# Second normalisation moved behind the up projection, early modulation products in row halves, and two groups of late modulation moved forward

## What is computed

```python
mod = cs @ w_mod[li] + b_mod[li]
sh_a, sc_a, gt_a, sh_f, sc_f, gt_f = [m[:, None, :] for m in jnp.split(mod, 6, axis=-1)]
h = rmsnorm(x, g_attn[li]) * (1.0 + sc_a) + sh_a
z = h @ w_in[li]
...
o = jnp.concatenate([oa.reshape(b, t, A_VW), ob.reshape(b, t, B_QW)], axis=-1) @ w_out[li]
x = x + gt_a * o
h2 = rmsnorm(x, g_ffn[li]) * (1.0 + sc_f) + sh_f
...
f, cnew = conv_ffn(h2, cstate, w_up[li], conv_w[li], conv_b[li], w_down[li])
...
x = x + gt_f * f
```

## Time and profile before

| | |
|---|---|
| median of the runs | 2734.76 us |
| the profiled execution's own time | 2732.63 us |
| its span, first to last instruction | 2730.9 us |
| TensorE matmul busy | 2620.5 us (96%) |
| VectorE (DVE) busy | 1558.8 us (57%) |
| ScalarE (ACT) busy | 957.5 us (35%) |
| GpSimd (POOL) busy | 544.7 us (20%) |
| mean granted TensorE clock | 0.985 of full speed |

### The profile page before, as it was taken

One profiled execution on the slowest core, in us unless ns is written; L12 is line 12 of the kernel. 1 busy time (PEld: TensorE's weight loads), 2 busy tenths in 40 slices (PEclk: granted clock), 3 DMA queues, 4 the chain that ended last, 5 costly groups with the idle time before them and its releaser, 6 DMA issues.

```text
span 2730.9 us, 50066 instructions
## 1 busy us (share of the span) xinstructions
PE 2620.5 (96%) x19783; PEld 2445.0 (90%) x19783; DVE 1558.8 (57%) x2873; ACT 957.5 (35%) x1974; POOL 544.7 (20%) x477
## 2 busy tenths in 40 slices
PE   7999999999999996999999999999999999999997
PEld 2268889898988995999999999999999999999997
DVE  1369889864457887854443544444444444345454
ACT  2236666654344336422222222222222222222224
POOL 1057777751003543310000000000000000000003
PEclk9999999999999998999999999999999999999998
DMA  8866556551216652533323232332332233232321
GB/s 291 294 202 184 184 174 183 182 145 51 66 40 188 169 165 70 155 108 93 93 79 93 81 90 82 90 88 83 93 92 72 87 93 91 81 93 79 93 93 69
DMA packets 416205, 324.91 MB, mean 119 GB/s; under 512 B 44410, under 2 KB 360218, under 8 KB 414880
## 3 DMA queue, kind: packets, MB, share of 16 engines
q1 hardware_dynamic: 410032, 302.55, 37.3%
q0 software_dynamic: 5248, 14.56, 1.7%
q10 hardware_dynamic: 688, 4.47, 0.4%
HBM read 307.67 MB, written 14.07 MB: 118 GB/s over the span
## 4 chain that ended last, share of the span: by engine, by line
PE 81%; DVE 8%; DMA 3%; issue 3%; POOL 2%; ACT 2%; SPq 1%; ACTq 0%; DVEq 0%; POOLq 0%
PE ps L1565 24%; PE ps L1567 23%; PE ps L1566 23%; DVE late_f L1261 3%; PE ps L1539 3%; PE ps L1654 2%; PE ps L1620 2%; DMA w_raw<-in_w_mod 2%; DMA w_raw<-in_w_out 2%; POOL oT L696 1%; PE ps L1638 1%; SPq L536 1%; DVE oT L1261 1%; ACT w_hi L798 1%; PE ps L1576 1%
## 5 line engine op out<-in xcount | busy, mean ns | idle before, releaser
L1565 PE MATMUL ps<-x_hi,w_hi 128*128 128x272 f32 x4480 | 1319.0, 294 | 53.7 <-DVE w_lo L1155 24.7
L1567 PE MATMUL ps<-x_hi,w_lo 128*128 128x272 f32 x4480 | 1302.9, 291 | 0.0
L1566 PE MATMUL ps<-x_lo,w_hi 128*128 128x272 f32 x4480 | 1293.5, 289 | 0.0
L1565 PEld LDWEIGHTS ps<-x_hi,w_hi 128*128 128x128 f32 x4480 | 850.3, 190 | 72.5 <-issue 32.2
L1566 PEld LDWEIGHTS ps<-x_lo,w_hi 128*128 128x128 f32 x4480 | 851.7, 190 | 0.0
L1567 PEld LDWEIGHTS ps<-x_hi,w_lo 128*128 128x128 f32 x4480 | 849.0, 190 | 0.0
L1155 DVE TENSOR_TENSOR w_lo<-w_raw,w_hi 128x1024 fp32r<-128x1024 f32 x368 | 459.0, 1276 | 341.0 <-ACT w_hi L798 340.6
L798 ACT ACTIVATE w_hi<-w_raw 128x1024 fp32r<-128x1024 f32 x368 | 375.6, 1056 | 715.3 <-PE ps L1567 574.1
L1566 PE MATMUL ps<-y_lo,w_hi 128*128 128x272 f32 x1408 | 407.2, 289 | 0.0
L1565 PE MATMUL ps<-y_hi,w_hi 128*128 128x272 f32 x1408 | 405.8, 288 | 0.0
L1567 PE MATMUL ps<-y_hi,w_lo 128*128 128x272 f32 x1408 | 405.0, 288 | 0.0
(11 more groups left out here) (194 smaller groups left out, 2081.6 us busy)
## 6 DMA issues: line engine op xcount, KB each, us to landing
w_raw<-in_w_mod SPq DMA_DIRECT2D x192, 512.0 KB, 4.6
w_raw<-in_w_up SPq DMA_DIRECT2D x176, 512.0 KB, 4.4
w_raw<-in_w_down SPq DMA_DIRECT2D x88, 512.0 KB, 4.7
w_raw<-in_w_in SPq DMA_DIRECT2D x56, 512.0 KB, 3.9
w_raw<-in_w_in SPq DMA_DIRECT2D x32, 256.0 KB, 3.7
w_raw<-in_w_out SPq DMA_DIRECT2D x16, 512.0 KB, 5.5
w_raw<-in_w_out SPq DMA_DIRECT2D x64, 128.0 KB, 3.9
x_transposed<-xT SPq DMA_DIRECT2D x4, 1088.0 KB, 8.1
```

What stands on the lines that cost most here:

```text
L1565: pe.matmul(out[:, 0:n], hi_w, hi_x, start=first, stop=False)
L1566: pe.matmul(out[:, 0:n], hi_w, lo_x, start=False, stop=False)
L1567: return pe.matmul(out[:, 0:n], lo_w, hi_x, start=False, stop=last)
```

## The change

Three parts.

**Second normalisation deferred.** RMSNorm multiplies each token by one number, so it commutes with the product over channels. `x_hi` and `x_lo` now hold the two parts of x1 * scale, without the token's factor, and TensorE begins with `w_up` at once. The shift is two more columns of `x_hi` and `x_lo`: the second token half of every `w_up` tile streams 274 columns for 272. DVE multiplies by the token's factor when it takes the product out of PSUM (`evict`, in place of ACT's `u_copy`), and ACT adds the shift's product per channel (`add_shift`). Scales come to stand at tile `SCALE_AT`, 72. Sum of squares, root and reciprocal run beside the first `w_up` tiles; POOL has no part any more. In a hidden step, DVE's order changes too: `lo` of the next step's chunks and two `down_out` come before the second `conv`.

**Late groups moved.** 12, 3 and 1 groups stand in the mixer, the output stage and the head of the channel layer, for 10, 4 and 2. The tiles over which `LATE1` is spread stay the same.

**Early products in row halves.** Each of the 128 products of the head becomes two, on partitions 0 to 63 and 64 to 127, into two banks. ACT copies 1024 elements out for 512; `group_columns` makes 8 fp32 products that add the two halves, for 4 transposes. The transposes of x have one pair of banks for two.

```diff
-LATE1 = 10 * LPG
-LATE2 = 4 * LPG
-LATE3 = 2 * LPG
+LATE1 = 12 * LPG
+LATE2 = 3 * LPG
+LATE3 = LPG
...
-        HEAD_LATE[_j, _q] = [LATE1 + LATE2 + 4 * _j + 2 * _q + _i for _i in range(2)]
+        HEAD_LATE[_j, _q] = [LATE1 + LATE2 + 2 * _j + _q]
...
-        x_hi = on(ctx, "x_hi", [P, KT, T], F32R)
-        x_lo = on(ctx, "x_lo", [P, KT, T], F32R)
+        x_hi = on(ctx, "x_hi", [P, KT, T + 2], F32R)
+        x_lo = on(ctx, "x_lo", [P, KT, T + 2], F32R)
...
-                act.activation(mod_rows[g % 2][:, :], bank(7 - g % 2)[0:2, :], ACT.Copy).then_inc(e_ev, 1)
+                act.activation(mod_rows[g % 2][:, :], bank(6 - 2 * (g % 2), 2)[0:2, :], ACT.Copy).then_inc(e_ev, 1)
...
+            def x1_hi(kt, h):
+
+                act.wait_ge(g_free, ZH + 2 * kt + h + 1)
+                for a, n, g in PIECES[h]:
+                    ins = act.activation(x_hi[:, kt, a:a + n], x1[:, kt, a:a + n], ACT.Copy,
+                                         scale=mod[:, SC_F + kt, g:g + 1])
+                ins.then_inc(n_hi, 1)
...
+            def add_shift(x, J):
+
+                act.wait_ge(u_ev, J * 4 + (2 * x + 2))
+                for a, n, g in ((0, TP, 0), (TP, TS, 1)):
+                    u = ext[x][:, a + 2 + 2 * g:a + 2 + 2 * g + n]
+                    ins = act.activation(u, u, ACT.Identity, bias=u_shift[x][:, g:g + 1])
+                ins.then_inc(u_sh, 1)
...
+            def x1_lo(kt, h):
+
+                dve.wait_ge(n_hi, 2 * KT + KT * h + kt + 1)
+                for a, n, g in PIECES[h]:
+                    ins = dve.scalar_tensor_tensor(out=x_lo[:, kt, a:a + n], in0=x1[:, kt, a:a + n],
+                                                   scalar=mod[:, SC_F + kt, g:g + 1],
+                                                   in1=x_hi[:, kt, a:a + n].bitcast(F32),
+                                                   op0=ALU.mult, op1=ALU.subtract)
+                ins.then_inc(x_ok, 1)
...
+            for kt in range(KT):
+                x1_lo(kt, 1)
             inverse(1, n2_rstd[:, :])
-            dve.wait_ge(mod_ok, KT // EGT + 1)
-            normalise()
-            dve.wait_ge(x_ok, 4 * KT)
...
+            def evict(x, J):
+
+                first = isinstance(J, int) and J == 0
+                for h in range(2):
+                    dve.wait_ge(u_done, J * 4 + (x + 2 * h + 1 if first else 2 * x + h + 1))
+                    b = bank(2 * x + h)
+                    if h:
+                        dve.tensor_copy(u_shift[x][:, :], b[:, H0:H0 + 2])
+                    for a, n, g in PIECES[h]:
+                        c = a - HALF[h][0]
+                        ins = dve.tensor_tensor(ext[x][:, a + 2 + 2 * g:a + 2 + 2 * g + n], b[:, c:c + n],
+                                                n2_rstd[:, a:a + n], ALU.mult)
+                    ins.then_inc(u_ev, 1)
...
                 for t in range(EGT):
-                    mm = pe.transpose(bank(5)[:, 2 * t:2 * t + 2], mod_rows[g % 2][0:2, P * t:P * t + P],
-                                      ident[0:2, 0:2])
+                    for u in range(2):
+                        mm = pe.matmul(bank(2)[:, 2 * t:2 * t + 2],
+                                       mod_rows[g % 2][0:2, EG * u + P * t:EG * u + P * t + P], ident[0:2, 0:2],
+                                       start=u == 0, stop=u == 1)
...
-                    mm = pe.matmul(bank(7 - g % 2)[0:2, :], cs[:, kt, :], w_raw[raw][:, EG * k:EG * k + EG],
-                                   start=kt == 0, stop=kt == KT - 1)
+                    for u in range(2):
+                        r = slice(64 * u, 64 * u + 64)
+                        mm = pe.matmul(bank(6 - 2 * (g % 2) + u)[0:2, :], cs[r, kt, :],
+                                       w_raw[raw][r, EG * k:EG * k + EG], start=kt == 0, stop=kt == KT - 1)
...
-            sum_squares(1, n2_acc)
-            pe.wait_ge(g_free, ZH + OH)
-
...
             for h in range(2):
                 up(0, (0, None), 0, (h,))
                 up(0, (0, None), 1, (h,))
+                if h == 0:
+                    sum_squares(1, n2_acc)
```

More of the change, by code:

```diff
@@ L344, in build @@
         lam = [on(st0, f"lambda{i}", [P, A_DK]) for i in range(4)]
-        mod_rows = [on(st0, f"mod_rows{i}", [2, EG]) for i in range(2)]
+        mod_rows = [on(st0, f"mod_rows{i}", [2, 2 * EG]) for i in range(2)]
         rows = on(st0, "rows", [P, 9, P])
@@ L376, in build @@
         cv = [on(st3, f"cv{i}", [P, T + 2]) for i in range(2)]
+        n2_rstd = on(st3, "n2_rstd", [P, T])
+        u_shift = [on(st3, f"u_shift{i}", [P, 2]) for i in range(2)]
         n2_st = ExitStack()
-        n2_sq, n2_acc, n2_rstd = [on(n2_st, f"n2_{x}", [P, T]) for x in ("sq", "acc", "rstd")]
+        n2_sq, n2_acc = [on(n2_st, f"n2_{x}", [P, T]) for x in ("sq", "acc")]
         n2_st.close()
@@ L407, in build @@
         st3.close()
-        h2_t, h2_h = (lambda i, b=b: b[i % 2][:, H0 * (i // 2 % 2):H0 * (i // 2 % 2) + H0] for b in (cv, ext))
         f_sq, f_sum = cv, ext[1][:, 0:T]
@@ L913, in _ @@
                                     else OUT_COUNT[6 * kt + 5])
-                        act.activation(x_hi[:, kt, :], oT[:, kt, :], ACT.Copy).then_inc(n_hi, 1)
+                        act.activation(x_hi[:, kt, 0:T], oT[:, kt, :], ACT.Copy).then_inc(n_hi, 1)
                 if pt is not None:
@@ L951, in _ @@
                     late_mul(n)
+            act.wait_ge(g_free, ZH)
+            act.activation(x_hi[:, :, shift], mod[:, SH_F:SH_F + KT, :], ACT.Copy).then_inc(sh_hi, 1)
             for hf in range(ZH, ZH + OH):
@@ L1020, in hidden @@
                                 late_mul(n)
-                    act.wait_ge(c_gate, J)
-                u_copy(0, 0, J * 4 + 1)
-                u_copy(0, 1, J * 4 + (3 if first else 2))
+                act.wait_ge(u_done, J * 4 + (3 if first else 2))
                 if first:
@@ L1028, in hidden @@
                 hi_ffn(at(5))
-                if not first:
-                    act.wait_ge(c_val, J)
-                u_copy(1, 0, J * 4 + (2 if first else 3))
-                u_copy(1, 1, J * 4 + 4)
+                add_shift(0, J)
+                act.wait_ge(u_done, J * 4 + 4)
                 if has_down:
@@ L1035, in hidden @@
                     hi_ffn(at(7))
+                add_shift(1, J)
                 act.wait_ge(c_gate, J + 1)
@@ L1392, in lo_ffn @@
                 lo(n, n % NR, SC0 + n if i is None else i * LOOP_CHUNKS + (SC0 + n))
-            for n in range(4):
-                lo_ffn((n, None))
+            for hf in range(ZH, ZH + OH):
+                n, h = (hf - ZH) // 2, hf % 2
+                if hf + 2 < FC0:
+                    lo_early(hf + 2)
+                elif h == 0:
+                    lo_ffn((0, None))
+                    lo_ffn((1, None))
+                else:
+                    dve.wait_ge(mod_ok, KT // EGT + 1)
+                    for kt in range(KT):
+                        x1_lo(kt, 0)
+                if h == 0 and n % 4 == 0:
+                    dve.wait_ge(xr[n // 4], 16)
+                dve.wait_ge(g_done, hf + 1)
+                ins = gated(n, h, out_bank(hf), GT_A)
+                (late_out(hf) or ins).then_inc(g_free, 1)
+                if hf == SCALE_AT:
+                    dve.wait_ge(g_free, hf + 1)
+                    scales(SC_F, KT, KT)
+                    dve.wait_ge(sh_hi, 1)
+                    dve.tensor_tensor(x_lo[:, :, shift], mod[:, SH_F:SH_F + KT, :], x_hi[:, :, shift].bitcast(F32),
+                                      ALU.subtract).then_inc(sh_lo, 1)
+                for x in late_of(hf, 0, 1):
+                    for c in x:
+                        late_sum(c)
+                if hf == FC0 - 1:
+                    lo_ffn((2, None))
+                    lo_ffn((3, None))
+                if h:
+                    dve.wait_ge(g_free, hf + 1)
+                    add_square(n, x1, n2_sq[:, :], n2_acc[:, :])
@@ L1728, in up @@
                         pe.wait_ge(u_ev, J * 4 + (2 * x + h - 3))
+                    else:
+                        pe.wait_ge(g_free, ZH + OH - 3 + 2 * x + h)
+                    if h:
+                        pe.wait_ge(sh_lo, 1)
+                        n += 2
                     for kt in range(KT):
```

115 lines of the change are left out of this document (30 added, 85 removed).

## The result

The changed kernel takes 2741.05 us (median of 10 runs, 2737.99 to 2744.77); the kernel before, run beside it, 2735.24. The ratio is 1.0022, with an interval of 1.0013 to 1.0030: **slower by 0.2%**, 6 us, where 2723 had been predicted, 12 faster. The time is inside the range, on the other side of no change.

The account below looks back on a forecast made before the run. TensorE was taken as the bound nearly everywhere, with DVE nearly full in the mixer. 2732.6 - 39 + 3 - 9 + 20 + 14 = 2721.6, with 2.1 for the median 2723.7, stated as 2723 us; range 2704 to 2745.

Parts of the forecast that it names:

- Deferral, -39: Head of the channel layer: deferred normalisation with one late group less takes 112.5 us for 153.0; gain 39, bounds 28 and 43.
- step 1: Hidden step in the channel layer's head: TensorE stalls 3 us for its weights, with 2.5 us left for value-half chunks.
- The three tests set for it: Channel layer's head: first w_up matmul within 0.5 us of the last w_out, no low clock there, 112 us for 153.
- Output stage, -9: Output stage: one late group goes, saving late sums and part of the waits for w_lo; gain 9 us, bounds 2 and 14.
- Mixer, +20: Mixer: two more late groups, 38 us of DVE work, partly in idle time; cost 20 us, bounds 3.4 and 41.
- half of 33: Mixer: where DVE idles it waits for a chain and can partly work instead, so the cost was taken as 20 us.
- the 56 of the forecast: Mixer: a head's six tiles were to take 56 us for 53.
- the 59 that I had set as the mark: Mixer: the prediction was to count as wrong if a head's six tiles took 59 us or more.
- The first rival: Mixer goes over to DVE and POOL: 38 us of new DVE work against 35.8 idle, 41 for 20, 2744; chance 0.20.
- Row halves, +14: Head: halves run side by side and give nothing, columns cost 11 us more; cost 14 us, bounds 8 and 20.
- the rival of fast halves: Head: two row halves are faster than one whole product, -13 for +14, 2696 at best; chance 0.05.
- Two columns, +3: Channel layer's w_up tiles: second token half streams 274 columns for 272; cost 3 us, bounds 0 and 3.5.

Follow-up runs that it names:

- table_back: The changed kernel with late groups back at 10, 4 and 2 in mixer, output stage and head of the channel layer: 2725.39 us, ratio 0.9967.
- rows_546: The kernel before with rows of x_hi and x_lo of 546 elements for 544, nothing else: 2738.60 us in one run.
- one_pair: The kernel before with the transposes of x in one pair of PSUM banks for two, nothing else: 2739.96 us in one run.

## Why the prediction was wrong

**Deferral, -39: right.** Measured -44.1, against bounds of 28 and 43. Of it the deferral alone is 20.4 and the group 23.7. The sum was right more than its shares: I had put down most of the gain to the deferral and some 8 us (6.2 and 1.7) to the group. No wait for `x_lo` was left, the sum of squares was hidden, and only 2.3 us of waits remain of the 5.5 that I had kept for step 1 and its successors. The three tests set for it held: no gap, no low clock, 109 us against 112.

**Output stage, -9: right**, 10.7 measured. PE waits there 1.6 us for `w_lo`, where 6.6 stood.

**Mixer, +20: this is the step that failed**, "Where DVE idles today it waits for a chain, and can partly work instead, so I take half of 33". Measured 42.8 in tiles 0 to 47, just over my upper bound of 41, and 45.2 with the rest of the mixer. The sum had 38 us of new work on DVE, about half of it in idle time. The runs show 52.8 us of new busy time and 10.0 of it in idle time. Half of a range is no measurement, and the 33 of that half is not derived (halfway between the bounds is 22). Two things were missing. First, I priced DVE with its mean of before (1188 ns) though POOL's share rose with it; over tiles 0 to 47 the mean rose from 1202 to 1349, 172 x 0.147 = 25 us of DVE work that no new instruction accounts for. Second, I priced waits at their length, though in a stage at 1.00 each may cost a fall of the clock too: of TensorE's 42.8 us, 19.7 are new idle time and nearly as many the clock. A head's six tiles took 58.4 us (tiles 12 to 47 in 350.5) for 53.0 before: over the 56 of the forecast, and just under the 59 that I had set as the mark.

**The first rival was the right one**: "the mixer goes over to DVE and POOL", 2744, chance 0.20, deciding from 37 us. The result is 2741; that it came so near is partly luck, since the head cost 6 more and the loop 9 less than its sum had. I had written against it that idle DVE time is not all chained. The eleventh group bears that out, at 10 us, and the twelfth does not: the idle time is spent once. The engine that ran out is DVE, as the rival had it, with POOL as what makes it slow; that POOL's additions lengthen DVE's operations beyond the mean of before was in no price. I had also written that by the page a chunk moved out of stages where POOL is free costs more here, and that the trace agrees. It does not for this change: POOL works in the stages that the chunks left, and there the operation took 1542 ns for 1188 in the mixer.

**Row halves, +14: mechanism right, size short.** They run side by side, as the earlier trace rows said, and the columns cost 12.2 for the predicted 11. Entering the mode around the transposes of x cost nothing that the trace shows (their stretch takes 43.11 us for 39.96, and two groups' columns are 3.06 of it). The 20.1 came from 2.0 us more of waits for ACT's longer copy (0.5 predicted) and from the lower clock behind these and behind a wait for a load, which no term had; with less of the lower clock the same head cost 14.8 in table_back. The Trainium skill (TensorEngine Tiling (Array Packing), Theoretical Speedup) gives up to 2x where the contracted side is 64 or less. The trace agrees, if that is read against two halves one after the other: 64 half passes take 13.90 us, 32 whole ones 13.89. Against whole rows, which the head had before, it is no gain, so that I had read the page wrongly in the rival of fast halves.

**Two columns, +3: wrong in its reason.** The columns cost 0.7 to 1.8, the rows' other length 6.0 in rows_546, the part that I had left at "nothing here prices that". That the turns of the loop would shorten by 12.7 us, the clock's part among them, was in no term and no rival.

Put together, the profiled execution took 2740.6 us where the sum said 2721.6. The 19.0 are 25.2 in the mixer, 6.1 in the head and 3.5 at tiles 72 and 73 (clock 0.84; one_pair, with the mixer of before, takes 26.7 us there as well, so it need not be the change's), less 5.1 for the deferral, 1.7 for the output stage and 9.0 for columns and loop.

**The better version.** The parts differ in sign: deferral -27, eleventh group -14 net, twelfth group and row halves each a loss. Eleven, four and one groups with whole rows take 2694.6 us, 1.5% below the kernel before.

## What to carry to other kernels

Work moved into a stage where an engine is nearly full fits until its idle time is spent, and then costs at least its whole length, and more by what two engines that work at once take from each other; measure one unit of it before moving two. Here the eleventh group cost 10 us and the twelfth 32. When several parts go in together, run each alone: here one part's gain hid that two others lost.

Cutting an engine's work to a few elements in a few instructions tells what that work costs a stage. Read it with the busy time of the other engines beside it: here the cut on POOL gave most, and with it went 19.6 us of DVE's time. And follow a wait back to the last thing that the late engine itself stood for before naming its cause.
